# A mixture-of-experts kernel: expert rounds of two blocks hold the weights in TensorE, and every round ends with its own second product

## What is computed

```python
top_vals, top_idx = lax.top_k(logits, TOP_K)              # 4 of 32 experts for each of 1024 tokens
...                                                       # rows sorted by expert, in blocks of 128
def expert_block(args):
    x_i, e = args                                         # 128 rows of one expert
    gu = x_i @ w_gate_up[e] + b_gate_up[e]                # 1024 -> 2048
    gate, up = jnp.split(gu, 2, axis=-1)
    gate = jnp.minimum(gate, SWIGLU_LIMIT)
    up = jnp.clip(up, -SWIGLU_LIMIT, SWIGLU_LIMIT)
    act = (up + 1.0) * (gate * jax.nn.sigmoid(SWIGLU_ALPHA * gate))
    return act @ w_down[e] + b_down[e]                    # 1024 -> 1024
...
y = jax.ops.segment_sum(yb * w_buf[:, None], tok_buf, num_segments=N + 1)[:N]
out = rmsnorm(x + gt2 * y, final_norm_g)
```

## Time and profile before

| | |
|---|---|
| time, median of 3 executions | 2965.39 us (2964.68 to 2966.34) |
| the profiled execution: its own time / its span | 2963.74 us / 2962.1 us |
| PE busy | 2679.7 us, 90% of the span |
| PE weight loads (PEld) | 2148.4 us, 73% |
| DVE busy | 1852.9 us, 63% |
| ACT busy | 1512.6 us, 51% |
| POOL busy | 316.2 us, 11% |
| HBM, mean over the span | 222 GB/s |

### The profile page before, as it was taken

How to read it: one execution, slowest core, us unless ns; L and a number is a source line. 1 busy time by engine, 2 the same in 40 slices (tenths; PEclk the granted TensorE clock), 3 DMA queues, 4 the chain that set the end, 5 groups by cost and what they waited for, 6 DMA issues and landing times. The chain is left out here.

```text
span 2962.1 us, 42755 instructions
## 1 busy us (share of the span) xinstructions
PE 2679.7 (90%) x12623; PEld 2148.4 (73%) x12624; DVE 1852.9 (63%) x2747; ACT 1512.6 (51%) x2198; POOL 316.2 (11%) x376
## 2 busy tenths in 40 slices
PE   4999799987889489999999999999999999999993
PEld 4888677765668367787878778777887787778771
DVE  4332154535556588566676865887658868776855
ACT  5221144433432177455565755776457757565741
POOL 0000011110002211110111101111111111111100
PEclk7999899997899699999999999999999999999995
DMA  6652222112343379668686986898668969876966
GB/s 244 232 192 79 95 84 75 63 54 79 131 153 135 136 267 334 198 215 291 213 278 212 358 274 211 282 339 286 215 215 280 337 202 355 288 254 209 355 205 209
DMA packets 431080, 639.53 MB, mean 216 GB/s; under 512 B 28034, under 2 KB 346676, under 8 KB 430884
## 3 DMA queue, kind: packets, MB, share of 16 engines
q1 hardware_dynamic: 402080, 562.46, 55.7%
q0 software_dynamic: 27712, 71.96, 9.1%
q10 hardware_dynamic: 1220, 4.21, 0.3%
HBM read 594.31 MB, written 64.73 MB: 222 GB/s over the span
## 5 line engine op out<-in xcount | busy, mean ns | idle before, releaser
L2443 DVE TENSOR_TENSOR e_gu_lo<-gu_raw,e_gu_hi 128x1024 fp32r<-128x1024 f32 x564 | 681.1, 1221 | 160.5 <-ACT e_gu_hi L2315 159.4
L82 PE MATMUL e_pgu<-e_gu_hi,e_x_hi 128*128 128x512 f32 x1568 | 643.5, 410 | 7.7 <-DVE e_x_lo L2473 5.7
L84 PE MATMUL e_pgu<-e_gu_hi,e_x_lo 128*128 128x512 f32 x1568 | 616.8, 393 | 0.0
L83 PE MATMUL e_pgu<-e_gu_lo,e_x_hi 128*128 128x512 f32 x1568 | 614.4, 392 | 0.0
L2315 ACT ACTIVATE e_gu_hi<-gu_raw 128x1024 fp32r<-128x1024 f32 x564 | 581.5, 1057 | 64.0 <-DMA gu_raw<-in_w_gate_up_dram 31.3
L84 PEld LDWEIGHTS e_pgu<-e_gu_hi,e_x_lo 128*128 128x128 f32 x1568 | 295.1, 188 | 64.5
L2449 DVE TENSOR_TENSOR e_dn_lo<-dn_raw,e_dn_hi 128x1024 fp32r<-128x1024 f32 x280 | 333.4, 1220 | 9.7 <-ACT e_dn_hi L2321 9.7
L82 PEld LDWEIGHTS e_pgu<-e_gu_hi,e_x_hi 128*128 128x128 f32 x1568 | 296.6, 189 | 54.2 <-issue 8.5
L83 PEld LDWEIGHTS e_pgu<-e_gu_lo,e_x_hi 128*128 128x128 f32 x1568 | 296.9, 189 | 46.2
L82 PE MATMUL e_pdn<-e_dn_hi,e_a_hi 128*128 128x512 f32 x784 | 308.9, 394 | 22.7 <-DVE e_a_lo L2477 21.2
L84 PE MATMUL e_pdn<-e_dn_hi,e_a_lo 128*128 128x512 f32 x784 | 305.8, 390 | 0.0
(11 more groups left out here) (411 smaller groups left out, 4047.8 us busy)
## 6 DMA issues: line engine op xcount, KB each, us to landing
gu_raw<-in_w_gate_up_dram SPq DMA_DIRECT2D x572, 512.0 KB, 6.2
dn_raw<-in_w_down_dram SPq DMA_DIRECT2D x142, 1024.0 KB, 9.5
wada_later<-in_w_ada_dram SPq DMA_DIRECT2D x32, 512.0 KB, 3.9
gu_bias<-hidden_bias SPq DMA_DIRECT2D x42, 256.0 KB, 7.6
win_raw<-in_w_in_dram POOLq DMA_DIRECT2D x5, 2048.0 KB, 10.9
proj_by_token<-out_stage SPq DMA_DIRECT2D x32, 256.0 KB, 2.8
wg_raw<-in_w_in_dram POOLq DMA_DIRECT2D x16, 512.0 KB, 4.9
gates_transposed<-g_stage POOLq DMA_DIRECT2D x32, 256.0 KB, 2.3
```

What stands on the lines that cost most here:

```text
L82: pe.matmul(out, a[0], w[0], start=first, stop=False)
L83: pe.matmul(out, a[0], w[1], start=False, stop=False)
L84: return pe.matmul(out, a[1], w[0], start=False, stop=last)
L2443: dve.tensor_tensor(gu_lo[:, b, 2 * j:2 * j + 2], gu_raw[:, b, 2 * j:2 * j + 2].rearrange("p k g n -> p k (g n)"), gu_hi[:, b, 2 * j:2 * j ...
```

## The change

Double rounds get a gate-up product of another form. PE now holds 128 x 128 pieces of the weights and streams the tokens of both blocks, 256 columns, past them. A unit is now half a chunk's hidden features (tile `t`) of both blocks: 48 matmuls of 256 columns in place of 24 of 512. The result comes out with hidden features on the partitions, so there are no transposes of the activations, and the bias is one value for each partition, which ACT adds with its two passes (`e_bias`, L2374 and L2375); bias matmuls, `gu_bias`, its loads and DVE's additions are gone from doubles. The bias columns are made in the routing phase, with 16 transposes and one copy, instead of a store to DRAM. The second product of a unit (`down_both`) takes one tile for both slots, again 12 matmuls of 512 columns, so the results of both slots are complete only at the end of the round. `e_a_hi` and `e_a_lo` have two buffers.

Singles and doubles now end with their own last second product. In the last unit of a single the pieces stand in another order. The last round loads nothing for a round behind it, and `b_down`, `final_g` and two tiles of the residual are loaded before the expert phase ends, into the space of `gu_raw`.

```diff
@@ phase_route
@@ tensor
+            pe.wait_ge(bias_up, 1)
+            for j in range(2 * KT):
+                rows = slice(j // KT * 2 * NE, (j // KT * 2 + 1) * NE)
+                ins = pe.transpose(pb[:, j // KT, j % KT], braw[rows, j % KT * P:(j % KT + 1) * P], m.ident[rows, rows])
+            ins.then_inc(bias_turned, 1)
...
@@ phase_experts, sync
-                    if two and c < CH - 1:
-
-                        wait_apart(sp, with_bias, U + 2 * c + 2)
-                        bs(here, c + 1, (c + 1) % 2)
-
                     for half in range(2):
                         wait_apart(sp, gu_lo_done, QG * q4 + QG * (c + 1) + (half + 1) * QG // 2)
-                        gu(here if c == 0 else there, (c + 3) % CH, (c + 1) % 2, half)
+                        if c == 0 or not final:
+                            gu(here if c == 0 else there, (c + 3) % CH, (c + 1) % 2, half)
+                        else:
+                            sp.sem_inc(gu_in[(c + 1) % 2][half], 32)
...
+            wait_apart(sp, gu_lo_done, 16 * n + 4)
+            sp.dma_start(m.c_bd, m.b_down[0]).then_inc(once_in, 16)
+            sp.dma_start(m.c_gf, m.final_g.rearrange("(a d) -> a d", a=1).to_broadcast([P, D])).then_inc(once_in, 16)
+            for t in range(2):
+                sp.dma_start(m.c_x2[:, t], m.x2[t * P:(t + 1) * P, :]).then_inc(once_in, 16)
+            wait_apart(sp, once_in, 64)
...
@@ tensor
+            def down_both(n, b, q, blocks, c, t):
+
+                pe.wait_ge(a_lo_done, n + 2)
+                pe.wait_ge(dn_lo_done, KD * q + t + 1)
+                if c == 0 and t == 0:
+                    pe.wait_ge(y_out, blocks)
+                for s in (1, 0):
+                    for half in range(2):
+                        cols = slice(half * N, (half + 1) * N)
+                        ins = three(pe, p_dn[:, s, cols], (a_hi[:, b, s], a_lo[:, b, s]), (dn_hi[:, c % 2, t, cols], dn_lo[:, c % 2, t, cols]),
+                                    c == 0 and t == 0, c == CH - 1 and t == KD - 1)
                 ins.then_inc(dn_done, 1)
...
-                        ins = three(pe, p_gu[:, l % 2].rearrange("p g n -> p (g n)"), (x_hi[:, s, k], x_lo[:, s, k]),
-                                    (gu_hi[:, c % 2, k], gu_lo[:, c % 2, k]), k == 0, k == KT - 1)
+                        else:
+
                             for g in range(2):
+                                cols = slice(g * FC + t * P, g * FC + (t + 1) * P)
+                                ins = three(pe, p_gu[:, l % 2, g], (gu_hi[:, c % 2, k, cols], gu_lo[:, c % 2, k, cols]),
+                                            (x_hi[:, k].rearrange("p s n -> p (s n)"), x_lo[:, k].rearrange("p s n -> p (s n)")),
+                                            k == 0 and g == 0, k == KT - 1 and g == 1)
...
-                    after_first(pe, r, l, lambda: down(n - 1, q4 + (pc if l else -1), B + 2, pc, ps))
+                    if l:
+                        second(n - 1, l - 1, pc, 1 - ps)
                     if s == 0 and c in (1, 2):
                         turn_x(r + 1, 2 * c - 2)
-
-            total, n = rounds(pe, body)
-            turn_a(total - 1)
-            down(total - 1, 4 * n - 1, 0, CH - 1, 0)
+                if two:
+                    pe.sem_inc(a_turned, 2 * CH)
+                    pe.sem_inc(pick_used, 1)
+                else:
+                    turn_a(n)
+                second(n, l, c, t)
...
@@ scalar
+                    act.activation(sg[:], p_gu[:, l % 2, 0], ACT.Gelu_apprx_sigmoid, bias=bcol[:, tile:tile + 1])
+                    act.activation(gb[:, 0], p_gu[:, l % 2, 1], ACT.Identity, bias=bcol[:, KT + tile:KT + tile + 1]).then_inc(swished, 1)
...
                 if two:
-                    evacuate(n - 1, 1, B, 2 * r + 2)
+                    evacuate(n, 1, B, 2 * r + 2)
...
@@ vector
                     if not two:
                         todo = [("g", 0), ("g", 1), ("g", 2), ("g", 3), ("d", 0), ("d", 1)]
+                        if c == CH - 1:
+
+                            todo = todo[0:2] + todo[4:6] + todo[2:4]
...
                     if (c, s) == (CH - 1, 0):
+                        piece()
                         low_x(r + 1, 0)
-                        if not by_pe(two, c):
-                            with_biases(n, c, l % 2, r)
+                        if two:
+                            low_x1_half(r + 1, 0)
+                        else:
+                            piece()
+                        activate(n, l, two)
                         low_x(r + 1, 1)
-                        activate(n, l % 2, by_pe(two, c))
+                        low_a(n, l, two)
```

More of the change, by code:

```diff
@@ L2104, in units @@
                 yield l, c, s, s == 0, seq[l - 1]
-        def by_pe(two, c):
-            return not two or c == 0
         def after_first(eng, r, l, body):
@@ L2152, in body @@
-                if not two:
-                    sp.sem_inc(bias_in[0], 16)
-                    sp.sem_inc(bias_in[1], 32)
-            total, n = rounds(sp, body)
+                    if c < 2 or not final:
+                        dn(here if c < 2 else there, (c + 2) % CH, c % 2)
+                    else:
+                        sp.sem_inc(dn_in[c % 2], 16)
+            n = sp.value_load(m.rounds[0:1, 0:1], min_val=1, max_val=MAX_ROUNDS)
+            end = sp.value_load(m.rounds[0:1, 1:2], min_val=0, max_val=MAX_ROUNDS)
@@ new lines, in _ @@
+            with sp.Fori(0, end) as r:
+                U = sp.snap(entry(sp, r, 3, 4 * (MAX_ROUNDS * SLOTS)))
+                two = entry(sp, r, 2, 1)
+                with sp.If(two > 0):
+                    body(r, U, True)
+                with sp.Else():
+                    body(r, U, False)
+            U = sp.snap(entry(sp, end, 3, 4 * (MAX_ROUNDS * SLOTS)))
+            two = entry(sp, end, 2, 1)
+            with sp.If(two > 0):
+                body(end, U, True, True)
+            with sp.Else():
+                body(end, U, False, True)
@@ L2396, in piece @@
                                 if j == 0:
-                                    act.wait_ge(dn_done, n + 1)
+                                    act.wait_ge(dn_done, n if two and c else n + 1)
                                 dn_piece(r, c, j)
```

204 lines of the change are left out of this document (108 added, 96 removed).

## The result

The changed kernel takes 2990.78 us (median of 4, 2986.88 to 2995.21) against 2965.03 us (median of 4): a ratio of 1.0087, 95% interval 1.007 to 1.0105. It is slower, by 26 us where I had forecast 10. The profiled execution took 2986.88 us, with a span of 2984.8 us, 22.7 us more than the span before.

What follows compares the result with a forecast made beforehand. PE alone was taken to bound doubles, and a ring of PE, ACT, DVE and weight loads singles. Expert phase +15 and end -6 gave +9 to +10 us on 2963.74; median forecast 2975 us, range 2953 to 2994.

Steps and rivals of the forecast that it cites:

- PE work of a double: TensorE's matmul work in a two-block round, claimed to fall by 0.8, from 69.8 to 69.0 us; 14 doubles give -11.
- the spacing: Time between starts of 256-column gate-up matmuls in two-block rounds, taken as 0.1175 us, between 0.1135 and 0.1225.
- The end of a round: Now serial: from H, the last gate-up product's end, PE's round work ends after 5.7 us in doubles, 7.3 in singles.
- Single after single: One-block round behind another: later end, earlier next unit, 40.1 us against 40.34; -0.3 x 12 = -4 us.
- Double after double: Two-block round behind another: PE waits 1.9 to 2.1 us for results held by a scatter; +1.2 x 5 = +6 us.
- Single after double: One-block round behind a two-block one: late weight pieces, PE waits 2.8 us at transposes; +1.6 x 8 = +13 us.
- The end: After the last round: first result +2.8 us, scatter without extra loads -4.7, constants loaded ahead -3.9; sum -5.8 us.
- Rival 2: Late start fills idle time in singles after doubles, scatters land sooner, singles gain: -10 us, 2955 to 2960; chance 0.19.
- Rival 5: PE's grown loop code no longer stays on the core, 2.0 us stall in 34 rounds: +70, 3045; chance 0.04.
- Rival 4: Weight loads show behind short matmuls: at 0.1225 us each +27, 3002; wholly unhidden +285, 3260; chance 0.04.

Runs made afterwards that it cites:

- the order of the second product: Kernel after, with the 12 matmuls of each second product reordered so those with `e_a_lo` come last: 1.0061 of the kernel before, 2985.3 us.
- the end alone: Kernel before with only the program's end changed (no loads for a nonexistent round, constants and residual tiles loaded ahead): 0.9978 of the kernel before, 2959.03 us.
- the repeat: The kernel after, unchanged, run once more on the same chip as the runs beside it: 1.0092 of the kernel before, 2992.64 us.
- The narrower matmuls: Kernel after with each 256-column gate-up matmul of doubles split into two of 128, one per block: 1.2471 of the kernel before, 3696.69 us.
- the pieces ahead: Kernel after with three of a round's first four weight pieces treated at the previous round's end, before `e_y` on ACT: 0.9947 of the kernel before, 2950.73 us.
- one piece ahead: Kernel after with each round's first weight piece treated at the previous round's end, before `e_y` on ACT: 1.0013 of the kernel before, 2969.71 us.
- the pieces of the second product first: Kernel after, with a single's last unit treating the second product's weight pieces first and DVE one fewer before the clamp: 1.0254 of the kernel before, 3041.77 us.

## Why the prediction came out as it did

The direction, the place of the largest loss and the range (2953 to 2994) held; the size was 10 us where it is 26. That the total is off by only 14 to 16 us is in part luck, as a step that was too high made up for others that were too low. By its steps:

- **PE work of a double** (69.0 us forecast; 69.3 from H to H with the wait and the branch at the end, before any wait for `e_y`): measured 70.11 between doubles. The mis-sized term is the spacing, 0.1175 forecast, 0.1207 measured (the mean of 5,250 pairs of starts), 384 x 0.0032 = 1.2 us a double; the other terms came out 0.4 us too high. A pair of bias matmuls between wide neighbours was too short a sample. It is the +0.8 of a double after a single.
- **The end of a round**: H + 5.7 and H + 7.3 forecast, 5.97 and 7.5 measured from the start of the last matmul, some 0.1 and 0.2 less from its end. Right.
- **Single after single**: -0.3 forecast (its own terms give -0.24), 0.0 measured. The mechanism was right: the end's wait is the next head's wait, as the order of the second product shows.
- **Double after double**: this step failed. I had ACT wait for slot 1's scatter, 10.7 us, and PE for ACT. In the trace slot 0's `e_y` starts 7.6 us behind the end of slot 1's in four of the five (8.6 in the first), in its place in ACT's order, and the scatter has landed by then; the only `e_y` that waits for a scatter is the very last. The 11.5 us that I read as "hardly later than it may" were ACT's order too in four of the five, where those scatters had landed after 10.3 to 10.5 us (in the fifth, of 70.20 us, after 12.1, and ACT waited 0.6 us), and the landing times that I took were those of scatters beside weight loads, from which the change moved them away. In four of the five the forecast was 1.0 us each too high (+1.2 against +0.25). The rest of the 7 us is the first of the five (73.66 to 71.25); the end alone, which has the old rounds, took 71.67 there too, so most of that isn't an effect of the new form.
- **Single after double**: the wait of 2.8 us was right (2.9, the same pieces in the same order). What I left out is what follows a wait on PE: a lower granted clock for 3 us and more, 1.4 to 1.7 us in six of eight. The forecast had such a round at 39.9 + 1.6 = 41.5 us, and the two without the lower clock take 41.6. So 9 of the 10 us that the step was short are the clock. It helped that the sum had no late load in it: before, five of the eight (39.75 to 40.84 us) had ACT wait 2.1 to 3.6 us for a load of `gu_raw`, and after none has. The profiled execution of the repeat has three such rounds at 44.4 us with longer stretches of the low clock, so it is one source of the spread of this kernel's times, 2987 to 2995.
- **The end**: -5.8 forecast, -6.4 measured, 3.0 - 4.7 - 4.7. The sum was right; the cause that I gave for the scatter was not.

So the forecast was short by 4 (singles after singles), 7 (the spacing) and 10 (singles after doubles), and 7 too high in doubles after doubles: 14 us for the profiled execution. The median is 3 us further off than that execution. Rival 2 had its chance in that waits hide behind a later start: it happened for the scatter, and didn't for the row of pieces. Rival 5 didn't happen in this kernel: the one stall at a head, in the second double, fell from 2.0 to 0.9 us. The narrower matmuls, with 768 instructions more, show that it was near. Rival 4 happened at its small end: 0.1207, under its 0.1225.

The change's parts are worth keeping apart. With the pieces ahead the new form is 0.5% faster than before. What it removes from DVE and its transposes isn't what makes it so: a double is 0.25 us longer than before after a double and 0.8 after a single. The gains are the end (-6), singles after doubles (39.9 to 38.5 us, -11) and singles after singles (40.34 to 39.97, -4), less +7 in doubles after singles. The end gains as much on the kernel before, and no run puts pieces ahead there, so how much of the rest the old form would have gained with them isn't known.

Not settled: when a wait is followed by the lower clock. Behind waits of 1.7 us it never was (8 rounds with one piece ahead); behind the 2.0 us at the head of the first double after a double, in the kernel before, it was; behind 2.7 us in 5 of 8 (the second product in another order), behind 2.9 to 3.0 in 6 of 8 in the kernel after and in 7 of 8 in its repeat, and behind 3.4 to 5.1 in 11 of 12 (the pieces of the second product first). One round with three pieces ahead (42.07 us, a single after a single) has such a stretch with no wait over 1.0 us in the 5 us ahead of it. The lengths alone don't tell the rounds apart.

## What to carry to other kernels

When work is moved to the end of a stretch, list what stands behind it on the engine that consumes it, and look for work of the next stretch that could go ahead: here three pieces ahead of one result turned +26 us into -15. Price a wait on TensorE together with the clock behind it: here waits of 2.7 us and more had it in most rounds, at 1.4 to 2.8 us each. Halving a matmul's columns pays little when each has weights of its own: 128 columns took 0.1115 us and 256 took 0.1207. And count the weight loads as instructions when a loop's body grows, and look at the instruction queue: 131 packets in place of none came with stalls of 4.4 to 5.0 us.

## What the runs showed that I had not expected

A matmul with 128 x 128 weights of its own starts 0.1115 us behind the one ahead with 128 columns, 0.1207 with 256, 0.227 with 512. An indirect scatter of 128 rows lands in 6.9 to 7.3 us behind its source's end in slot 1 of the doubles after, with no weight load issued in the first 4.7 us, and in 10.3 to 12.1 in the same place before, with three issued by 2.9 us; the other scatters after, but for the last, take 9.1 to 12.5 us. Two weight pieces asked for before their load had landed cost 51 us, with 5.0 us of waiting for a load at the longest. And PE can be busy all the time at the lower granted clock for 44 us, with 128-column matmuls, behind a stall of 4.6 us.
